# Head norm in four steps, the second weight tile prepared later, and unnormalised rows in differential attention

## What is computed

```python
q_d, k_d = _rope(dq), _rope(dk)                       # differential: 4 heads x 2 halves of 32
q_g = _rope(_rms(gq, g_gqa_q), rope_large)            # grouped: 8 query heads of 64
k_g = _rope(_rms(gk, g_gqa_k), rope_large)            # grouped: 2 key heads of 64
...
def _sdpa(q, k, v, scale):
    s = jnp.einsum('bhgqd,bhkd->bhgqk', q, k).astype(jnp.float32) * scale
    p = jax.nn.softmax(s, axis=-1).astype(v.dtype)
    return jnp.einsum('bhgqk,bhkd->bhgqd', p, v)
...
d = od[:, :, 0] - lam.astype(od.dtype) * od[:, :, 1]   # differential: half 0 minus lam times half 1
d = _rms(d, g_diff_sub) * (1.0 - lam_init)
```

## Time and profile before

| | |
|---|---|
| three timed runs | 2435.92 us in the median, 2435.25 to 2446.86 |
| the profiled execution | 2444.03 us, span 2442.3 us in the trace |
| granted clock over the span | 0.955 |
| PE busy | 2197.6 us (90%) |
| DVE busy | 1729.4 us (71%) |
| ACT busy | 1147.7 us (47%) |
| POOL busy | 52.5 us (2%) |

### The profile page before, as it was taken

One profiled execution on the slowest core, in us unless ns is written; L12 is line 12 of the kernel. 1 busy time (PEld: TensorE's weight loads), 2 busy tenths in 40 slices (PEclk: granted clock), 3 DMA queues, 4 the chain that ended last, 5 costly groups with the idle time before them and its releaser, 6 DMA issues.

```text
span 2442.3 us, 38098 instructions
## 1 busy us (share of the span) xinstructions
PE 2197.6 (90%) x14746; PEld 1974.9 (81%) x14746; DVE 1729.4 (71%) x3414; ACT 1147.7 (47%) x1937; POOL 52.5 (2%) x65
## 2 busy tenths in 40 slices
PE   3998799999999999989987979799989988797998
PEld 2987789999987778979865756799889978567997
DVE  5667668889987787788866665577766675664554
ACT  2643344545554444454454445444454445354444
POOL 1000000000000000000000000000000000000000
PEclk9999989999999999999987889899999998898999
DMA  7648646664467887768721110377767753103564
GB/s 276 201 143 281 203 132 199 205 208 141 147 200 254 264 264 244 272 225 256 253 87 39 61 44 18 120 247 244 238 205 257 252 164 123 52 1 102 183 189 131
DMA packets 137987, 435.04 MB, mean 178 GB/s; under 512 B 15376, under 2 KB 38160, under 8 KB 137296
## 3 DMA queue, kind: packets, MB, share of 16 engines
q1 hardware_dynamic: 109440, 396.93, 50.5%
q10 hardware_dynamic: 25776, 23.97, 2.9%
q0 software_dynamic: 2592, 11.70, 1.3%
HBM read 418.91 MB, written 13.63 MB: 177 GB/s over the span
## 4 chain that ended last, share of the span: by engine, by line
PE 54%; DVE 18%; DMA 11%; issue 11%; ACT 5%; POOL 1%; ACTq 0%; DVEq 0%; POOLq 0%; SPq 0%
PE bk L1676 51%; DVE SPL L1101 5%; DMA TMP<-kept 4%; PE bk L1682 3%; DMA RAW<-in_peer 3%; DMA RAW<-in_win 3%; ACT SPL L761 2%; DVE RAW L1135 2%; DVE R L1101 2%; DVE R L1110 1%; DVE TMP L1101 1%; ACT R L763 1%; DVE ST L1116 1%; POOL ST L663 1%; DVE EXT L1135 1%
## 5 line engine op out<-in xcount | busy, mean ns | idle before, releaser
L1101 DVE TENSOR_TENSOR SPL<-RAW,SPL 128x1024 fp32r<-128x1024 f32 (+1 forms) x614 | 747.5, 1223 | 367.8 <-ACT SPL L761 366.2
L761 ACT ACTIVATE SPL<-RAW 128x1024 fp32r<-128x1024 f32 (+1 forms) x614 | 644.9, 1054 | 618.4 <-PE bk L1676 278.9
L1676 PE MATMUL bk<-HH,SPL 128*128 128x256 f32 x3840 | 747.9, 288 | 25.7 <-DVE SPL L1101 16.5
L1676 PEld LDWEIGHTS bk<-HH,SPL 128*128 128x128 f32 x3840 | 621.2, 194 | 33.8 <-issue 14.8
L1676 PE MATMUL bk<-SPL,WHL 128*128 128x512 f32 x2328 | 554.5, 392 | 15.2 <-DVE WHL L1101 11.2
L1676 PE MATMUL bk<-HL,SPL 128*128 128x256 f32 x1920 | 547.2, 285 | 0.0
L1676 PEld LDWEIGHTS bk<-SPL,WHL 128*128 128x128 f32 x2328 | 428.0, 188 | 109.3 <-issue 21.4
L1676 PEld LDWEIGHTS bk<-HL,SPL 128*128 128x128 f32 x1920 | 372.7, 194 | 2.3
L1676 PE MATMUL bk<-SPL,HH 128*128 128x256 f32 (+1 forms) x1664 | 314.8, 291 | 32.4 <-DVE SPL L1101 21.1
L1676 PEld LDWEIGHTS bk<-SPL,HH 128*128 128x128 f32 x1664 | 268.5, 199 | 41.5 <-issue 23.2
L761 ACT ACTIVATE R<-bk 128x512 f32<-128x512 f32 (+4 forms) x358 | 176.0, 503 | 204.4 <-PE bk L1676 180.2
(11 more groups left out here) (129 smaller groups left out, 2010.7 us busy)
## 6 DMA issues: line engine op xcount, KB each, us to landing
RAW<-in_peer SPq DMA_DIRECT2D x256, 512.0 KB, 4.8
RAW<-in_ada SPq DMA_DIRECT2D x144, 512.0 KB, 4.8
RAW<-in_ffn SPq DMA_DIRECT2D x132, 512.0 KB, 4.2
RAW<-in_win SPq DMA_DIRECT2D x96, 512.0 KB, 4.5
RAW<-in_ffd SPq DMA_DIRECT2D x66, 512.0 KB, 4.4
RAW<-in_wout SPq DMA_DIRECT2D x32, 512.0 KB, 4.4
kept<-TMP ACTq DMA_DIRECT2D x88, 128.0 KB, 3.4
TMP<-kept ACTq DMA_DIRECT2D x66, 128.0 KB, 5.5
```

The costliest lines, as they stand in the source:

```text
L761: ins = e.activation(out, in_, func, bias=bias, scale=scale)
L1101: e.tensor_tensor(out, a, b, op).then_inc(*dve.up(*points))
L1676: ins = e.matmul(out, lhsT, rhs, start=start, stop=stop, skip_group_check=True)
```

## The change

Three edits come together.

First, `gn` is cut into `gn_a` (squares, sums, mean), `gn_b` (reciprocal root, scaling, gains), `gn_c` (first half of the turn) and `gn_d` (second half, copy of the keys). In the woven parts the projections 4, 5, 6 now come first and 7 and 0 last, and the four steps stand between the later ones. The transposes of `kk` and `pg` come ahead of `qa`. In `(1, 1)` the four steps stay together.

Second, for the projections in `WOVEN` (5 of (0, 1), 8 of (0, 0), 5 of (1, 0)) the tile that belongs to the step's second weight tile is prepared later: on ScalarE behind the step's copy out of PSUM, on VectorE behind the maximum of the next unit.

Third, in the differential heads `nm` leaves half 0 as it is and scales half 1 by lambda x sum 0 / sum 1; the division by sum 0 is made once on the result, in `df_a`. The products `av` of these heads hold the values still and stream the rows (output 64 x 256), as the other heads do; two new steps `ad` copy the results out, and `dq` transposes them back (4 transposes).

```diff
-    rest = [("pj", l, s, 7), ("pj", l, s, 0), ("scl", l, s, "k"), ("scl", l, s, "q")]
-    rest += [("pj", l, s, 4), ("lr1", l, s, "k"), ("pj", l, s, 5), ("lr2", l, s, "k", 0), ("lr2", l, s, "k", 1), ("kpe", l, s)]
-    rest += [("lr1", l, s, "q"), ("pj", l, s, 6), ("gn", l, s)]
+    rest = [("pj", l, s, j) for j in (4, 5, 6)] + [("gn_a", l, s), ("pj", l, s, 7), ("scl", l, s, "k"), ("gn_b", l, s)]
+    rest += [("pj", l, s, 0), ("scl", l, s, "q"), ("lr1", l, s, "k"), ("gn_c", l, s)]
+    rest += [("lr2", l, s, "k", i) for i in range(2)] + [("lr1", l, s, "q"), ("gn_d", l, s), ("kpe", l, s)]
     rest += [("tr", l, s, "ka", i) for i in range(2)] + [("lr2", l, s, "q", i) for i in range(2)] + [("qpe", l, s)]
-    return first, rest + [("tr", l, s, n, i) for n in ("qa", "kk", "pg") for i in range(2)]
+    return first, rest + [("tr", l, s, n, i) for n in ("kk", "pg", "qa") for i in range(2)]
...
-        if 8 <= n < 48 and UNITS[n - 8][2:] == (1, 1) and UNITS[n - 8][0] != 1 and UNITS[n - 8][1] % 2:
-            out.append(("ao", l, s, head_of(n - 8) // 2 - 2))
-        out += [("df_a", l, s)] * (n == 24) + [("df_b", l, s)] * (n == 27) + [("dT", l, s)] * (n == 30)
+        if 8 <= n < 48 and UNITS[n - 8][2:] == (1, 1) and UNITS[n - 8][1] % 2:
+            out.append(("ad" if UNITS[n - 8][0] == 1 else "ao", l, s, head_of(n - 8) // 2 - 2))
+        out += [("dq", l, s)] * (n == 24) + [("df_a", l, s)] * (n == 25) + [("df_b", l, s)] * (n == 28) + [("dT", l, s)] * (n == 31)
...
+WOVEN = {("pj",) + a for a in [(0, 1, j) for j in (0, 4, 5, 6, 7)] + [(0, 0, j) for j in range(8)] + [(1, 0, j) for j in (0, 4, 5, 6, 7)]}
...
             for step in PLAN:
-                ahead = max([ahead] + [lead(n) for n in CHUNKS[step]])
-                while done < min(ahead, len(ORDER)):
-                    if IS_SPLIT[done]:
-                        split_hi(done)
-                    done += 1
+                later = CHUNKS[step][1:] if step in WOVEN else []
+                done = prepare(CHUNKS[step][:1] if later else CHUNKS[step], done)
                 act.stage = STAGE.get(step[0], "layer")
                 if step[0] in steps:
                     steps[step[0]](*step[1:])
+                done = prepare(later, done)
...
+                if step in WOVEN:
+                    now, later = now[:1], now[1:]
+                done = prepare(now, done)
                 dve.stage = STAGE.get(step[0], "layer")
                 if step[0] in steps:
                     steps[step[0]](*step[1:])
+                if step[0] == "as":
+                    done, later = prepare(later, done), []
...
+                if kind == 1 and u == 0:
+                    return
                 e.reciprocal(r, r).then_inc(*dve.up())
-                if kind == 1 and u == 1:
+                if kind == 1:
                     dve.wait_ge(dve.own, T.at("lam"))
-                    tt(r, r, lamc[:, l:l + 1], ALU.mult)
+                    stt(r, r, lamc[:, l:l + 1], q["RS"][:, n - 1:n], ALU.mult, ALU.mult)
...
+            def dq(l, s):
+                key, d = ("avd", l, s), v2(QS[(l, s)]["Yf"], 2)
+                b = take(key, SCORE[(l, s)])
+                pe.wait_ge(T.at("out", ("av", l, s, -1)))
+                blocks(b, [d[:, k, i * P:(i + 1) * P] for i in range(2) for k in range(2)], P, ("full", key))
```

More of the change, by code:

```diff
@@ L144, in qkv_steps @@
     out += [("pj", l, s, j) for j in ((4, 5, 6) if full else (6,))]
-    out += [("lr1", l, s, "k"), ("lr2", l, s, "k", 0), ("lr2", l, s, "k", 1), ("kpe", l, s), ("gn", l, s)]
+    out += [("lr1", l, s, "k"), ("lr2", l, s, "k", 0), ("lr2", l, s, "k", 1), ("kpe", l, s)]
+    out += [(n, l, s) for n in ("gn_a", "gn_b", "gn_c", "gn_d")]
     out += [("tr", l, s, "ka", i) for i in range(2)] + [("pj", l, s, 3)]
@@ L999, in lr1 @@
                 aT3 = v2(QS[(l, s)]["aT"][:, 0:kc * 256], kc)
-                act.wait_ge(T.at("full", key))
+                act.wait_ge(T.at("full", key), act.own)
                 if n == "q":
@@ L1171, in rope @@
                 tt(x2, x2, a4, ALU.add, *points)
+            def rope(x4, cs, sn, n, half, tmp, *points):
+                rope_a(x4, cs, sn, n, half, tmp)
+                rope_b(x4, cs, sn, n, half, tmp, *points)
             def top16(lists):
@@ L1521, in gn, with gn_b @@
                 mean_eps(ss, 64, "gn", l, s)
+            def gn_b(l, s):
+                hd, nh, ss, r, y = heads(l, s)
                 newton(r, y, ss, "gn", l, s)
@@ L1579, in df_a @@
                 key, d, sq, sd = ("avd", l, s), QS[(l, s)]["Yd"], DS[s][:, 0:512], stat(136, 8, s)
-                dve.wait_ge(T.at("full", key))
-                cp(d, v2(ps(*key), 2), ("out", key))
+                first = QS[(l, s)]["RS"][:, 0:16].rearrange("p (n u) -> p n u", u=2)[:, :, 0]
+                by_tile = stat(144, 8, s).rearrange("p (h i) -> p i h", i=2).unsqueeze(3).to_broadcast([P, 2, 4, 64])
+                e.reciprocal(stat(144, 8, s), first).then_inc(*dve.up())
+                dve.wait_ge(T.at("full", key), dve.own)
+                tt(d.rearrange("p i (h d) -> p i h d", d=64), v2(ps(*key), 2).rearrange("p i (h d) -> p i h d", d=64), by_tile,
+                   ALU.mult, ("out", key))
                 dve.wait_ge(dve.own)
@@ L1945, in av @@
                 pe.wait_ge(T.at("out", ("at", l, s, n)))
-                if g < 4:
-                    key = ("avd", l, s)
-                    b = take(key, VALUE[(l, s)][:1]) if g == 0 else ps(*key)
-                    for i in range(2):
-                        for k, v in enumerate(vals):
-                            end = i == 1 and k == last
-                            done = [("pv", l, s, g)] + [("full", key)] * (g == 3)
-                            mm(b[:, i * 256 + 64 * g:i * 256 + 64 * g + 64], pt[:, k, i * P:(i + 1) * P], v, k == 0,
-                               k == last, *(done if end else ()))
-                    return
                 key = ("av", l, s, g // 2 - 2)
-                b = ps(*key) if g % 2 else take(key, VALUE[(l, s)][::-1])
+                b = ps(*key) if g % 2 else take(key, VALUE[(l, s)][:1] if g < 4 else VALUE[(l, s)][::-1])
                 r = slice(64 * (g % 2), 64 * (g % 2) + 64)
```

75 lines of the change are left out of this document (49 added, 26 removed).

## The result

The changed kernel takes 2447.6 us in the median (2441.3 to 2456.4), the kernel before 2436.7 (2430.6 to 2446.9), each over 20 runs: ratio 1.0042, 95% interval 1.0030 to 1.0053. That is 11 us slower, where 19 us faster was forecast. The profiled execution took 2452.7 us, with a span of 2450.9.

The account below looks back on a forecast made before the run. TensorE was taken to idle 18 to 22 us per woven part, mainly in one wait for VectorE's `gn`; -8 -8 -5 +2 = -19 us from 2444.0 gave 2425, less 8.1 for the median: 2417 us, range 2396 to 2434.

Parts of the forecast that it names:

- the likeliest mechanism: Woven parts: VectorE becomes the bound, its work strung on a chain; 2417 us in all, 5 in 10.
- three or four of 3 to 6 us: Woven parts: these waits for VectorE replace the 15 us one, first ahead of `lr2`, last ahead of `ka` transposes.
- The terms -8 and -8: Woven parts of (0, 0) and (1, 0): splitting `gn` gains 8 us each, (0, 0) taking 73 instead of 81.2.
- The 64 us to VectorE's end: Woven part of (0, 0): VectorE is through at 22 + 38 + 4 = 64 us.
- the tail: Woven parts of (0, 0) and (1, 0): from VectorE's last part to unit 16, taken as 9 us.
- 3 or less: Woven part of (0, 0): VectorE's wait for high halves of weight tiles falls from 9.5 us to this.
- The term -5 for (0, 1): Woven part of (0, 1): 7.2 us wait gained, less two high halves of 1.05 us, so 5 us gained.
- I cost it at nothing: Later tile on ScalarE: copy and high half ahead of the next exponential stay hidden behind scores and maximum, cost zero.
- The slower rival: TensorE waits 2.3 us after each of 18 projections, exponentials delayed; 22 us slower, 2458 us, 1 in 10.
- 0.6 behind each: Rows behind the woven parts: 0.6 us more, listed among the signs that the forecast is right.
- the rival that the prediction calls the third and names second: Gap only breaks up: three waits of 4 to 5 us each drop the clock; 5 less, 2431 us, 2 in 10.
- the 6.8 us at half clock: (0, 1): time at 0.50 read behind a 3.5 us wait, used as the clock's price for each shorter wait.

Follow-up runs that it names:

- e9: Changed kernel plus unneeded products: 20 in two waits behind (0, 1), 36 ahead of the first `lr2` of (0, 0) and (1, 0); 2440.6 us, ratio 1.0008.
- e4: Changed kernel without the later tile (steps and differential heads only); 2440.5 us, ratio 1.0018.
- e12: Changed kernel with the old order and `gn` in one piece in (0, 1) only; 2442.4 us, ratio 1.0020.
- e2: Kernel before with only the later tile added; 2448.4 us, ratio 1.005.
- e6: Changed kernel without the later tile for projections 1, 2, 3 of (0, 0), which stand among the rows behind (0, 1); 2442.4 us, ratio 1.0021.
- e13: Changed kernel without the later tile in (0, 1) itself, keeping it elsewhere; 2454.7 us, ratio 1.0055.
- e17: Changed kernel with `kpe`, the `ka` transposes and `lr2 q` ahead of `gn_d` for s = 0 (some values come out wrong); 2444.1 us, ratio 1.0022.
- e14: Kernel before with steps and later tiles in (0, 0) and (1, 0) only, 14 unneeded products in (0, 1), old differential heads; 2435.0 us, ratio 0.9986.
- e3: Kernel before with only the differential heads edit; 2440.4 us, ratio 1.0009.
- e8: Changed kernel with 20 unneeded products in two TensorE waits in the rows behind (0, 1); 2437.8 us, ratio 1.0004.
- e11: Kernel before with 14 unneeded products ahead of unit 23's transposition in (0, 1); 2434.6 us, ratio 0.9982.

## Why the prediction was wrong

**The diagnosis held, and the likeliest mechanism up to the transposes of `ka`.** The 15 us wait went, and waits of 6.2 (ahead of `lr2`), 0.9, 1.8 (ahead of `ka`) and 2.2 us took its place, one and not three or four of 3 to 6 us. VectorE's load in the part of (0, 0) is 50.0 us as computed, and e9 shows that VectorE's chain is the bound up to `ka`.

**The terms -8 and -8 were mis-sized.** They measured -2.8 and -4.3 us by the stretches of the earlier trace rows, for which they were forecast (-4.0 and -5.5 from maximum to maximum). The 64 us to VectorE's end were right to 1 us, in part by luck: unit 6 reached VectorE after 23.2 us, not 22, and from there it took 39.7, not 42. The step that failed is the tail: "before, from the end of the wait to unit 16 it took 8.6 us", so 9. That was read behind the wait for `qa`, whereas the new last wait is ahead of `ka`, with `lr2 q` still to come: 15.5 us, which makes the part 78.4 us and not 73. The order of the queues already showed that both steps had moved. Waits for high halves fell to 5.0, not to 3 or less.

**The term -5 for (0, 1) had the wrong sign.** It came out as +6 in 01w and +12.5 in the rows behind (+7.6 and +10.6 by the stretches). The step took the 7.2 us wait as gained and charged two high halves of 1.05 us ahead of the squares. The waits only moved: TensorE idles 22.9 us of the woven part with the change and 22.5 before. VectorE's waits for the squares of norms grew by 11 us and not by 2 x 1.05, from 5.7 in three to 16.8 in three (the longest from 3.5 to 7.8):

```profile
DVE ST L1121 <- ACT R L766: 16.8, 3, 7.8
```

They are 11.9 us with the steps and no later tile (e4), and 10.9 with the later tile and no steps (e12). Half clock in 01w rose from 41 to 51 us, and TensorE's work there took the longer for it. e12 puts the steps' share in (0, 1) at 5 us of the total.

**"I cost it at nothing" failed for the later tile.** Alone it costs 12 us by the ratio and 10 between the medians (e2), within the change 7 (e4). The prediction asked whether ScalarE's exponential is late behind the high half in the woven parts. Within the change the cost lies elsewhere, at three projections in the rows behind (0, 1) (e6, e13), on which the prediction had no term: VectorE's low half of 1.22 us stands ahead of `nm` and `df_a`, TensorE waits 1.14 us longer, and the part is 3.9 us longer at equal half clock (e17 against e6) or 11.3 with more of it. Alone the tile also costs 3.1 us in the woven part of (0, 1), where the squares of norms are late again, and 2.1 in that of (0, 0); how its 10 to 12 us come about in full is not shown. The slower rival had the edit right and not the size: no wait stands behind each of the 18 projections.

**The heads** cost 1.1 us behind (0, 0) within the change (e14 gives it back) and 1.7 and 1.8 behind (0, 0) and (1, 0) alone (e3), where 0.6 behind each was forecast. In 01s they cost nothing (e3: 1.1 us less).

**The clock** was let in as a price of breaking up one wait in the latent parts, as the rival that the prediction calls the third and names second. The half clock between the wait and `ka` costs nothing there (e9); in the tail it may. It cost in (0, 1) and in its rows of 256 columns, which were nearly full and at whose clock the prediction had not looked. The reading for the 6.8 us at half clock was not exact either: the 3.5 us in the earlier trace rows are VectorE's wait; TensorE's own was 3.58 us and ended at 1239.38, and the clock fell at 1238.3, inside it. And the rival's sum counts 1 us for (0, 1) where 5 less 5 is nothing, which makes it 2432 and not 2431.

## What to carry to other kernels

When a step is moved, read in the order of the queues what stands behind each wait before and after, and measure the tail from that landmark; a tail taken from another wait misses whole steps. An edit that only delays work by one instruction should be priced wherever it applies, above all where the engine that waits is nearly full: here a wait longer by 1.1 us came with a part longer by 3.9 us in one profile and 11.3 in another. When a stage gets longer, look for another run that has the same instructions there: e17 shows that 7.4 us of what e6 seemed to prove can come and go with the clock. Where a trace shows half clock over a stretch in which TensorE was busy throughout, look at the wait ahead of it and try unneeded products in that wait: a small edit that can tell a clock that sets the end (e8, e11) from one that does not (e9).
